# Two reordered stretches of a two-layer trunk: the opening's query products, and the fillers of the double memory step

## The reference

```python
for layer in range(DEPTH):
    if layer < N_A_LAYERS:
        z = x @ a_w_in[layer]
        zu = gelu(z[..., :D_MIX]); zv = layer_norm(gelu(z[..., D_MIX:2*D_MIX]), ...)
        qm = z[..., 2*D_MIX:]                       # memory queries
        mix = chunked_sgu(zu, zv, a_w_s[layer], a_b_s[layer])
    else:
        kvf = x @ kv_w                              # shared keys, values, forget gate
        z = x @ b_w_q[j]; q, qm = z[..., :D_MIX], z[..., D_MIX:]
        mix = fox_attention(q, k_sh, v_sh, logcum)
    mo = memory_attention(qm, mk, mv)               # softmax(qm mk^T / 8) mv
    y = concatenate([mix, mo], -1) @ w_o[layer]
    x = layer_norm(ALPHA * x + y, ...)
    x = layer_norm(ALPHA * x + square(relu(x @ w_up[layer])) @ w_down[layer], ...)
```

## Time and profile before

| | |
|---|---|
| median of three runs | 1162.04 us |
| the profiled execution, its own time | 1161.27 us |
| its span (first to last instruction) | 1159.5 us |
| PE busy | 1138.4 us (98%) |
| DVE, ACT, POOL busy | 623.4, 480.4, 131.9 us |
| mean granted clock of TensorE | 0.998 |
| PE's share of the chain that ended last | 84% |

### The profile page before, as it was taken

The page is one execution under the profiler, slowest core; times in us unless marked ns, Lnnn a source line. Parts: engine busy times, 40 slices in busy tenths (PEclk is TensorE's granted clock), DMA queues, the critical chain, the costliest instruction groups (busy, mean ns, idle before and its releaser), DMA issues.

```text
span 1159.5 us, 16356 instructions
## 1 busy us (share of the span) xinstructions
PE 1138.4 (98%) x5792; PEld 960.7 (83%) x5792; DVE 623.4 (54%) x1070; ACT 480.4 (41%) x830; POOL 131.9 (11%) x157
## 2 busy tenths in 40 slices
PE   9999999999999999999999999999999999999997
PEld 7888898888888888889778888788888888888886
DVE  7668657444233444355687787746454233444226
ACT  6556357343122343225765556536443212334120
POOL 4100064000000000233301001046000000000000
PEclk9999999999999999999999999999999999999999
DMA  9223423233333333332212122133333333333232
GB/s 366 91 73 90 128 73 110 75 106 91 108 92 91 92 106 92 103 97 81 66 45 66 55 57 71 44 102 92 86 95 99 101 90 90 91 93 106 91 114 87
DMA packets 164230, 110.36 MB, mean 95 GB/s; under 512 B 4690, under 2 KB 156242, under 8 KB 163668
## 3 DMA queue, kind: packets, MB, share of 16 engines
q1 hardware_dynamic: 163460, 106.28, 30.5%
q10 hardware_dynamic: 720, 3.41, 0.8%
HBM read 105.48 MB, written 4.19 MB: 95 GB/s over the span
## 4 chain that ended last, share of the span: by engine, by line
PE 84%; DVE 8%; ACT 4%; DMA 2%; issue 2%; POOL 0%; DVEq 0%; ACTq 0%; SPq 0%; POOLq 0%
PE proj L593 67%; PE pv L593 3%; PE sc L593 2%; PE proj L988 2%; PE sc L988 2%; PE pv L988 2%; PE tr L988 2%; DVE w_lo L1603 2%; PE tr L644 1%; DMA w_raw<-in_w_o 1%; ACT w_hi L1205 1%; DVE split_lo L1603 1%; DVE sc L1672 1%; DVE probs L1691 0%; ACT x L1396 0%
## 5 line engine op out<-in xcount | busy, mean ns | idle before, releaser
L1603 DVE TENSOR_TENSOR w_lo<-w_raw,w_hi 128x1024 fp32r<-128x1024 f32 (+1 forms) x168 | 210.9, 1256 | 157.3 <-ACT w_hi L1205 109.4
L593 PE MATMUL proj<-x_hi,w_hi 128*128 128x512 f32 (+1 forms) x752 | 291.5, 389 | 2.4 <-ACT x_hi L1387 1.2
L593 PE MATMUL proj<-x_hi,w_lo 128*128 128x512 f32 (+1 forms) x752 | 287.0, 383 | 0.0
L593 PE MATMUL proj<-x_lo,w_hi 128*128 128x512 f32 (+1 forms) x752 | 282.5, 383 | 0.0
L1205 ACT CAST w_hi<-w_raw 128x1024 fp32r<-128x1024 f32 x153 | 159.8, 1045 | 205.0 <-PE proj L593 199.6
L593 PEld LDWEIGHTS proj<-x_hi,w_hi 128*128 128x128 f32 x752 | 141.4, 188 | 29.6 <-issue 1.5
L593 PEld LDWEIGHTS proj<-x_hi,w_lo 128*128 128x128 f32 x752 | 141.3, 188 | 28.2
L593 PEld LDWEIGHTS proj<-x_lo,w_hi 128*128 128x128 f32 x752 | 139.2, 188 | 24.9
L593 PE MATMUL proj<-h_hi,w_hi 128*128 128x512 f32 (+1 forms) x384 | 146.3, 381 | 0.4 <-DVE w_lo L1603 0.4
L593 PE MATMUL proj<-h_hi,w_lo 128*128 128x512 f32 (+1 forms) x384 | 146.0, 380 | 0.0
L593 PE MATMUL proj<-h_lo,w_hi 128*128 128x512 f32 (+1 forms) x384 | 146.0, 380 | 0.0
(11 more groups left out here) (382 smaller groups left out, 1776.0 us busy)
## 6 DMA issues: line engine op xcount, KB each, us to landing
w_raw<-in_w_up SPq DMA_DIRECT2D x64, 512.0 KB, 4.0
w_raw<-in_w_down SPq DMA_DIRECT2D x64, 512.0 KB, 3.6
w_raw<-in_w_o SPq DMA_DIRECT2D x16, 512.0 KB, 3.6
w_raw<-in_a_w_in SPq DMA_DIRECT2D x12, 512.0 KB, 3.2
w_raw<-in_kv_w SPq DMA_DIRECT2D x12, 512.0 KB, 3.9
w_raw<-in_b_w_q SPq DMA_DIRECT2D x8, 512.0 KB, 3.6
w_raw<-in_mem_w_kv SPq DMA_DIRECT2D x5, 512.0 KB, 3.6
x<-in_x SPq DMA_DIRECT2D x4, 512.0 KB, 10.4
```

The source lines that it names most:

```text
L593: last = pe.matmul(target, lhs, rhs, start=start and n == 0, stop=stop and n == len(terms) - 1)
L1603: return dve.tensor_tensor(target, whole, hi.bitcast(F32), ALU.subtract)
```

## The change

Opening, PE: units 4 and 5 go in six passes of eight matmuls, each with its own wait: unit 4's high and low weights x high trunk, unit 5's high and low weights x high trunk, then unit 4's high weights x low trunk (with the waits for the low trunk tiles) and unit 5's high weights x low trunk. ACT prepares unit 6 before it reads the query result of unit 4 and not after. DVE reads the second natural values and prepares unit 5 before the low trunk tiles 5 and 7, and prepares unit 6 before it reads unit 4's result.

Double memory step: filler 3 has one k tile and not three, filler 4 has three as before, filler 5 has four and not two. ACT reads the first pair's queries (`fox_head`) in round 3 and not 2, and prepares unit 98 in round 4 and not 3. DVE makes the queries' low parts (`fox_query`) in rounds 3 and 4 and not 2 and 3, and prepares unit 98 at the head of round 5 and not of round 3.

```diff
--- before.py
+++ after.py
@@ -824,7 +824,7 @@
 
                 mixing = b is not None and s.base < STEP_B
                 at = [0, 4, 6] if mixing else [0, 0, 4] if s.base == STEP_B else [0, 3, 6]
-                at += [8, 11, 14, 16, 18, 19, 21, 24]
+                at += [8, 9, 12, 16, 18, 19, 21, 24] if s.base == STEP_B else [8, 11, 14, 16, 18, 19, 21, 24]
 
                 def filler(n):
                     if b is not None:
@@ -1141,8 +1141,28 @@
                     pe.wait_ge(x_rest, X_REST.index(k) + 1)
                 else:
                     pe.wait_ge(x_ready, k + 1 - sum(n < k for n in X_REST))
-            opening_projection(Pos(B_AQ), Pos(G_AQ), x_hi, x_lo, lambda k: pe.wait_ge(x_hi_ready, k + 1), trunk_ready)
-            project(Pos(B_AQ + 1), Pos(G_AQ + 1), x_hi, x_lo)
+
+            def opening_queries():
+
+                def run(c, signal, part, side, each=None, start=False, stop=False):
+                    b, g = Pos(B_AQ + c), Pos(G_AQ + c)
+                    if start:
+                        wait(pe, proj_free[g.slot], g.half())
+                    pe.wait_ge(signal, b.base + 1)
+                    for k in range(KT):
+                        if each:
+                            each(k)
+                        last = pe.matmul(proj[g.slot][:, :], weights(b)[part][:, k], side[:, k], start=start and k == 0,
+                                         stop=stop and k == KT - 1)
+                    if stop:
+                        last.then_inc(w_used, 1)
+                run(0, w_hi_ready, 0, x_hi, lambda k: pe.wait_ge(x_hi_ready, k + 1), start=True)
+                run(0, w_split, 1, x_hi)
+                run(1, w_hi_ready, 0, x_hi, start=True)
+                run(1, w_split, 1, x_hi)
+                run(0, w_split, 0, x_lo, trunk_ready, stop=True)
+                run(1, w_split, 0, x_lo, stop=True)
+            opening_queries()
             pe.wait_ge(const_ready, 4)
             pe.wait_ge(mk_copied, 2 * MEMPAIRS)
             for s in range(2):
@@ -1311,7 +1331,7 @@
                 for u in range(8):
                     if mixing and u in (0, 3, 6):
                         prepare(b.plus(u // 3 + 1))
-                    if reading and u == (3 if double(s) else 4):
+                    if reading and u == 4:
                         prepare(b.plus(2))
                     if reading and u == 7:
                         prepare(b.plus(3))
@@ -1333,7 +1353,7 @@
                         last.then_inc(f_act, 1)
                     if mixing and u in (2, 5):
                         step_projection(s, b.plus(u // 3), g.plus(u // 3), u // 3)
-                    if reading and u == 2:
+                    if reading and u == (3 if double(s) else 2):
                         for head in range(2):
                             fox_head(b, g, 0, head)
                     if reading and u in (5, 6):
@@ -1508,8 +1528,8 @@
             trunk_hi(range(4, KT))
             natural_values(1)
             prepare(Pos(B_AQ + 1))
+            prepare(Pos(B_AV))
             memory_queries(Pos(B_AQ), Pos(G_AQ), 0)
-            prepare(Pos(B_AV))
             memory_queries(Pos(B_AQ + 1), Pos(G_AQ + 1), 1)
             for s in range(2):
                 pair_step(Pos(STEP_A + s), Pos(B_AV + 3 * s), Pos(G_AV + 3 * s))
@@ -1779,7 +1799,7 @@
                         prepare(b.plus(u // 3 + 1))
                     if reading and u == 0:
                         prepare(b.plus(1))
-                    if reading and u == (3 if double(s) else 4):
+                    if reading and u == (5 if double(s) else 4):
                         prepare(b.plus(2))
                     if double(s) and u == 0:
                         dve.wait_ge(f_step, 3)
@@ -1806,8 +1826,8 @@
                         natural_z(3 * s.base + u // 6)
                     if mixing and s.base and u == 1:
                         natural_z(2)
-                    if reading and u in (2, 3):
-                        fox_query(values, g, u - 2)
+                    if reading and u - double(s) in (2, 3):
+                        fox_query(values, g, u - double(s) - 2)
                     if reading and u == 6:
                         fox_key(values, g.plus(1), 0)
                 turned_probs(s, 6)
@@ -2031,12 +2051,12 @@
             trunk_rest(3)
             natural_values(0)
             prepare(Pos(B_AQ))
+            natural_values(1)
+            prepare(Pos(B_AQ + 1))
             trunk_rest(5)
             trunk_rest(7)
-            natural_values(1)
-            prepare(Pos(B_AQ + 1))
+            prepare(Pos(B_AV))
             memory_queries(Pos(G_AQ), Pos(Q_AQ), 0)
-            prepare(Pos(B_AV))
             memory_queries(Pos(G_AQ + 1), Pos(Q_AQ + 1), 1)
             for s in range(2):
                 pair_step(Pos(STEP_A + s), Pos(B_AV + 3 * s), Pos(G_AV + 3 * s))
```

## The result

The changed kernel takes 1165.87 us (median of 10, 1164.01 to 1166.81), the kernel before 1162.08 (median of 10); the ratio is 1.0031, 95% interval 1.0023 to 1.0040. The change makes the kernel slower: by 3.6 us by the ratio, by 3.8 by the two medians. The forecast was 3.3 us more, 1165.3 us. Its profiled execution took 1165.78 us, span 1164.0.

What follows compares the result with a forecast made beforehand. PE was taken to bound the kernel (busy 1138.4 of 1159.5 us), its waits paid in full. Opening -0.25, double-step waits +2.3 and clock +1.2 gave +3.3 us, 1165.3 us; own range 1164.4 to 1166.3, wider range 1162.4 to 1167.0.

Steps and rivals of the forecast that it cites:

- The opening's breaks go: Opening passes: PE's breaks on the low trunk and unit 5's low part vanish, pass 6 ending 1.2 us earlier.
- Bank 0 is late next and takes nearly all of it: Opening, ahead of unit 6: PE waits for bank 0 until 31.82, so of 1.2 us only 0.25 is kept.
- No gain up to scores 5, gap of round 3 gone: Double step: scores 5 start at 583.3, early scores 3 buy nothing themselves; the 1.05 us gap at 584.84 goes.
- The chain of five DVE instructions ahead of filler 6: Double step: unit 98's low part follows DVE's list, 4.8 us from scores 5, filler 6 at 588.1; +2.3 us in all.
- The clock: Behind the 3.9 us gap ahead of filler 6 PE returns at 1.2 GHz; +1.2 us, between nothing and 1.8.
- Covers: Moved work has its inputs in time, among it ACT's cast of unit 6 between 21.7 and 22.7; costs nothing.
- no fall of the clock: Rival for the double step: the same waits without the 1.2 us of half clock, 1164.1 us; chance 0.17.
- the opening gives all: Rival for the opening: bank 0 doesn't hold PE, the full 1.2 us is gained, 1164.4 us; chance 0.08.
- The faster rival: Double step: unit 98's low part there by 584.2, -1.4 us; 1160.4 (chance 0.08), or 1159.4 with the full opening (0.05).

Runs made afterwards that it cites:

- the filled gap: Changed kernel plus sixteen matmuls on constants in PE's gap ahead of filler 6 of the double step; 1164.02 us, ratio 1.0019 to the kernel before.
- the other order of passes: Kernel before with only the opening changed, unit 4's low-trunk pass moved ahead of unit 5's low-weight pass; 1160.69 us, ratio 0.9988 to the kernel before.
- the opening alone: Changed kernel with the double step's filler list and ACT's and DVE's rounds set back; 1162.07 us, ratio 0.9998 to the kernel before.
- the step alone: Kernel before with only the double step's changes (filler list, ACT's and DVE's rounds); 1165.58 us, ratio 1.0029 to the kernel before.
- both gains: Kernel before plus the opening with unit 4's low-trunk pass earlier and the double step's new filler list only; 1159.70 us, ratio 0.9973.

## Why the prediction was right

*The opening's breaks go*: right; no break in six passes. *Bank 0 is late next and takes nearly all of it*: right; forecast 31.82 and a gain of 0.25, measured 31.92 (0.13 of it was there before: the second pass starts at 21.70 against 21.57) and 0.23. That it is the bank is shown by the experiment that gives the hand-over one pass more of other work, not only by the row.

*No gain up to scores 5, gap of round 3 gone*: right (583.3 forecast, 583.14 measured, in a step that starts 0.19 earlier; transposes 583.8, measured 583.62).

*The chain of five DVE instructions ahead of filler 6*: right; 4.8 us from scores 5, measured 587.87 - 583.14 = 4.73, and the step's waits came to 2.3 as forecast.

*The clock*: right that it falls; the size was somewhat low, 1.2 taken against 1.44 by the filled gap (the upper bound was 1.8). What was taken off for PE's wait ahead of round 5's transposes was too much: the half-clock stretch lay mostly before scores 6, and DVE's chain starts only there.

Two readings behind this term were not sound, and that it came out near is in part luck. The row that priced it, 13 matmuls from 1.18 to 6.16, shows starts that are far apart, but the granted clock in the windows from 1.18 to 6.00 us of that trace is 1.00 throughout, so it is no row of the half clock; the row at 588.46 of the changed kernel is one, with 0.43 us from start to start. And 1.05 us is not the longest idle stretch of the kernel before that left the clock alone. Its timeline of PE has a longer one, with 1.00 before and behind it:

```profile
152.78 0.39 PE L593 MATMUL proj<-mix_hi,w_hi 128*128 128x256 f32 x1 [1.49 <-DVE w_lo L1603]
```

*Covers*: one was thinner than written. ACT's cast of unit 6 was forecast for 21.7 and waited 0.75 us for the transfer until 22.58; no one needed it before 26.39. The working had no row on that transfer.

Of the rivals, "no fall of the clock" was made by filling the gap (1.0019), and "the opening gives all" by the other order of passes. The faster rival, unit 98's low part in time, came true only where the orders of DVE and ACT were left alone: -1.43 in the trace, -1.4 forecast. As written it named one condition too few. It let the low part alone decide, and with the low part made earlier PE still waited 2.70 us, for the query that frees bank 0. The sum did have that query, as one link of its chain.

The Trainium skill ("TensorE: Matmul & The Clock Gate", section "HAM oscillation — how this bites in real kernels") says that a long enough wait of PE between bursts puts the array back to half rate. The traces agree for the middle of a kernel: gaps of 3.65 and 2.70 us brought 0.50 in all three profiled executions that have one left open. The 2.70 us is shorter than the waits that the section describes, and the fall in the layer norm, behind a gap of 0.44 us, is not of that kind.

Left open: what decides where the clock falls. The length of the gap ahead of it does not by itself: 1.49 us left it alone, 2.70 did not, the same 3.65 brought the fall at 588 in one execution and at 590 in another, and in the layer norm 0.44 us brought it in one execution and not in the next.

## What to carry to other kernels

When a pass that finishes an accumulation is moved back, look at who needs that bank next: the hand-over (here 2.8 us from the end of the last matmul to the next use, 29.1 to 31.92) must have that much other work behind it. When a preparation is moved back in an engine's list, add up the whole list between it and the wait that gates it; a wait moves with everything ahead of it. And look at the granted clock behind a PE gap of some microseconds: the gaps of 2.70 and 3.65 us here cost once as a wait, and once more, 0.8 to 1.4 us, as work at half clock behind them.

## What was not expected of the hardware

In the layer norm before the last MLP the granted clock fell in some profiled executions, the changed kernel's among them, though the PE gap ahead of it was only 0.44 us (the bracket of the row at 802.34). The same wait of 0.44 us stands in the kernel before, where the clock held. The stretch has groups of matmuls of one column (128x1, at 800.01), which the busy time counts like others; that they have to do with the fall is a guess that no run tests. The fall costs 1.0 us in the pair above and is in four of nine profiled executions: the changed kernel, the opening alone, the step alone and both gains. None of these shares a part of the change with all the others that the five without it lack, so it isn't laid to the change; why it falls in one execution and not in another was not tested.
